# RWKV scan: exponentials wait for less, seeds cross partition halves by transfers

## The chip, the cores and the metric

The kernel runs on one core of a Trainium2 chip. The metric is the device time of one execution in microseconds (us), from start to end, and the median of three runs is given. All data is f32. The core has a matrix engine (PE, whose weight loads are listed apart as PEld), a vector engine (DVE), a scalar engine (ACT), GpSimd (POOL) and SyncE (SP), which here only issues transfers. Each engine works through its own list of instructions in order, and the lists meet by semaphores.

## The reference, cut to what matters

The reference is one step of a four-layer diffusion backbone over 128 context tokens and 1024 latent tokens, width 1024. Layers 0 and 3 mix tokens by a bidirectional RWKV-7 scan, layer 1 by attention, layer 2 by a short convolution. Each layer begins with an RMS norm, scaled and shifted by columns made from a conditioning vector. The scan goes over all tokens, in both directions, for 16 heads with 64x64 states:

```python
def step(S, inp):
    r_t, w_t, k_t, v_t, kk_t, a_t = inp
    sa = jnp.einsum('bdhvk,bdhk->bdhv', S, -kk_t)
    S = (S * w_t[..., None, :] + sa[..., None] * (kk_t * a_t)[..., None, :]
         + v_t[..., None] * k_t[..., None, :])
    return S, jnp.einsum('bdhvk,bdhk->bdhv', S, r_t)
```

## The kernel before, in words

The build runs phase after phase with a barrier between them: `phase_open`, then for each layer its mixer and a boundary phase. The change touches `phase_open` and `phase_scan`; the scan runs twice, for layers 0 and 3.

**The scan.** It does not step token by token. It works on 36 pairs: a pair is one 128-token tile in each direction for two blocks of 128 channels, so four units (two directions, two blocks) of two heads each. Inside a tile the recurrence over 64 tokens is solved by inverting a triangular 64x64 matrix for each unit, head and half tile. The inverse is built by doubling in five levels, n = 2, 4, 8, 16, 32. Of pair q:

- the decayed operands are made ahead: DVE sums the log decays (`decay`, L1625) and subtracts (`decay_before`, L1631), ACT makes five exponentials (`exps(q, 0)` to `exps(q, 4)`, L1516), and DVE multiplies (`decayed_a` L1645, `decayed_b` L1653, `decayed_k` L1658, `decayed_r` L1663).
- `gram(q, t)` (PE, L1286) makes the products of keys with keys and queries, `masked` (DVE, L1677) keeps the triangle, and `pairs(q, t)` (DVE, L1671) puts the entries of the first doubling step into the tile `y1` (semaphore `y1_ok`, two per pair).
- from `y1` come two things. `seeds` (DVE, L1686) transposes its blocks into the tile `x`, from which `level_u(q, 1)` (PE, L1313) starts. `turned_seeds` (PE, L1297) moves its blocks across the two partition halves by eight half-size products with the identity into two PSUM banks, and `copy_seeds` (ACT, L1524) copies them into `xt` (semaphore `t1_ok`), from which `level_x(q, 1)` (PE, L1327) starts.
- level k: `level_u` (PE), `level_w` (DVE, L1698, keeps the entries of this level), `level_x` (PE, L1327), `copy_x` (ACT, L1520, semaphore `xa_ok`), `level_t` (PE, a transposition, L1338), `copy_t` (ACT, L1549, semaphore `xt_ok`).
- `tokens_v`, `tokens_bk` (PE, L1357, L1364) turn values and keys, `values` (PE, L1375) and `copy_values` (ACT, L1543) make a part of the right-hand side.

The states go along in a chain one pair behind: `chain_rhs` (PE L1393 and L1398, DVE L1711), `chain_sa` (PE L1414, ACT L1558), `chain_state` (PE L1425 and L1433, DVE L1736), `chain_y` (ACT, L1567) and the scalings (DVE, L1717).

**The order.** Each engine's list is one loop over q, written out by hand: in iteration q, PE, ACT and DVE do the levels of pair q, both steps of the chain of pair q-1 and the gram of pair q+1, and ACT and DVE prepare pair q+2. ACT's list has, in the first half of iteration q, this stretch:

```python
if chain:
    chain_sa(c, 0)
if nxt2:
    exps(q + 2, 0)
if here:
    copy_values(q)
    copy_x(q, 2)
if chain:
    chain_y(c, 0)
if nxt2:
    exps(q + 2, 1)
```

`exps(q, i)` for i below 4 waits until `decayed_r`, `decayed_a` and `decayed_k` of the pair before are done. Of these, `exps(q, 0)` writes into the tile `er`, which `decayed_r` reads; `exps(q, 1)` and `exps(q, 2)` write into `ab`, which `decayed_a` and the others read. On DVE the order is `decayed_r(q+1)`, `level_w(q, 2)`, `decayed_k(q+1)`, `decay_before(q+2)`, `decayed_a(q+1)`.

PE's list ends iteration q with `level_u(q, 5)`, `level_t(q, 4)`, `turned_seeds(q+1)`, and begins iteration q+1 with `chain_rhs`, `level_u(q+1, 1)`, `tokens_v`, `last_level_t` (L1347), `level_x(q+1, 1)`. ACT has `copy_seeds(q+1)` between `chain_y(c, 1)` and `exps(q+2, 4)`, ahead of `copy_t(q, 4)`. SP issues, in iteration q, the eight loads of pair q+3 (L1113, L1116, L1118, L1126; they wait for pair q+1's products of DVE), once the reload of `g.x` (q = 1, 4608 KB), and the stores of pair q-1's outputs (L1246: two in iterations whose pair is 4 to 19, one before, none after; where SP stores one or none, POOL adds the rest into memory, L1814). Line L1984, which the prediction uses for comparison, stands in the attention phase: eight transfers of 64 KB in a row from 16 partitions to 16 others, both ends in SBUF.

**The opening.** `phase_open` loads x in four parts. ACT squares its eight blocks (L264) into two buffers, PE adds them up over channels by 24 products with a tile of ones, which is loaded (`norm_matmuls`, L333), and each buffer is free when PE has read it. DVE and ACT turn the sums into 1/rms, DVE multiplies x by it (L306). In the same PE list, behind the norm, stand the products of the conditioning vector with the eight pieces of the first layer's weights (`ada_products`, L168; pieces loaded by L246), then a copy by ACT (L184), four transpositions (L176), a sum on DVE (L193, L201), and with these columns ACT and DVE scale and shift (L276, L316), which ends the phase.

Of the kernel before, what the change touches and what calls it, by code (L numbers as in the profile page):

```python
# [20 lines left out]
P = 128  # L21
# [7 lines left out]
CH = 3  # L29
# [182 lines left out]
def phase_open(nc, g, layer):  # L212
# [4 lines left out]
    ms, root, rstd = g.big[0][:, 0, :], g.big[0][:, 1, :], g.extra[:, 0:T]  # L217
    rest = g.arena[:, 2 * NB * T:4 * NB * T]
# [8 lines left out]
    with ExitStack() as ctx:  # L227
        sem = Sems(nc, ctx)
        cond_in, ident_in, ones_in, chan_in, next_in, set_ok, sig_ok, silu_ok = sem(
            "cond_in", "ident_in", "ones_in", "chan_in", "next_in", "set_ok", "sig_ok", "silu_ok")  # L230
        sq_ok, sq_used, ms_ok, root_ok, rstd_ok, tmp_ok, h_ok, h_vector_ok = sem(
            "sq_ok", "sq_used", "ms_ok", "root_ok", "rstd_ok", "tmp_ok", "h_ok", "h_vector_ok")
# [5 lines left out]
        @block.sync  # L238
        def _(sp):
            sp.dma_start(cond, io["cond"]).then_inc(cond_in, 16)  # L240
            n = NB // X_PARTS
            for i in range(X_PARTS):
                sp.dma_start(g.x[:, n * i:n * i + n, :], io["x"][:, n * i:n * i + n, :]).then_inc(x_in[i], 16)
            sp.dma_start(g.ones[:, :], io["ones"]).then_inc(ones_in, 16)
            for k in range(NB):
                sp.dma_start(pieces[k], io["w_ada"][0, k]).then_inc(piece_in[k], 16)  # L246
            sp.dma_start(g.ident[:, :], io["ident"]).then_inc(ident_in, 16)
            sp.dma_start(g.chan[:, :], io["chan"]).then_inc(chan_in, 16)
            sp.dma_start(g.head_ones[:, :], io["head_ones"]).then_inc(next_in, 16)
            for s in range(WSLOTS):  # L250
                sp.dma_start(g.slab[:, s, :], io["w"][mixer_slabs(layer) + s]).then_inc(next_in, 16)
            sp.wait_ge(next_in, 16 * (WSLOTS + 1))

        @block.scalar
        def _(act):
# [4 lines left out]
            for b in range(NB):  # L260
                act.wait_ge(x_in[b * X_PARTS // NB], 16)
                if b >= 2:
                    act.wait_ge(sq_used, b - 1)
                nc.scalar.activation(sq[b % 2], g.x[:, b, :], ACT.Square).then_inc(sq_ok, 1)  # L264
# [4 lines left out]
            act.wait_ge(set_ok, 4)  # L269
# [10 lines left out]
        @block.tensor  # L280
        def _(pe):
            pe.wait_ge(ones_in, 16)
            norm_matmuls(pe, g, sq, sq_ok, sq_used, 0)
            pe.wait_ge(silu_ok, 1)
            for k in range(NB):
                pe.wait_ge(piece_in[k], 16)
                mm = ada_products(pe, g, pieces[k], ROWS, k)
            mm.then_inc(rows_mm, 1)
            pe.wait_ge(ident_in, 16)
            pe.wait_ge(rows_sb, ADA_TILES)  # L290
            ada_turned(pe, g, rows, COLS).then_inc(cols_mm, 1)

        @block.vector
        def _(dve):
# [4 lines left out]
            dve.wait_ge(set_ok, 4)  # L299
            dve.wait_ge(sig_ok, 1)  # L300
            nc.vector.tensor_tensor(g.silu[:, :], cond, sig, op=ALU.mult).then_inc(silu_ok, 1)
            dve.wait_ge(sq_used, NB)
# [23 lines left out]


def norm_matmuls(pe, g, sq, sq_ok, used, banks):

    for b in range(NB):  # L330
        pe.wait_ge(sq_ok, b + 1)
        for c in range(CH):
            mm = pe.matmul(g.ps[:, banks + c, 0:CW], g.ones[:, :], sq[b % 2][:, c * CW:(c + 1) * CW],  # L333
                           start=b == 0, stop=b == NB - 1)
        mm.then_inc(used, 1)
# [804 lines left out]
def phase_scan(nc, g, j):  # L1140
# [46 lines left out]
    with ExitStack() as ctx:  # L1187
# [3 lines left out]
        gram_mm, init_mm, u_mm, x_mm, t_mm, rhs_mm, sa_mm, st_mm, y_mm, tok_mm, rv_mm = sem(  # L1191
            "gram_mm", "init_mm", "u_mm", "x_mm", "t_mm", "rhs_mm", "sa_mm", "st_mm", "y_mm", "tok_mm", "rv_mm")
        g_ok, y1_ok, x_ok, xa_ok, t1_ok, xt_ok, w_ok, rhs_ok, sav_ok, sum_ok, start_ok, half_ok, end_ok, y_ok, tok_ok, tokv_ok, rv_ok = sem(
            "g_ok", "y1_ok", "x_ok", "xa_ok", "t1_ok", "xt_ok", "w_ok", "rhs_ok", "sav_ok", "sum_ok", "start_ok", "half_ok", "end_ok", "y_ok", "tok_ok",
# [3 lines left out]
        ahead_in = sem("ahead_in")  # L1198
        v_in = [sem(f"v_in{i}") for i in range(4)]
# [15 lines left out]
        def _(sp):  # L1215
# [12 lines left out]

            sp.dma_start(w_all, io["scan_const"][:, lay["w"]:]).then_inc(w_in, 16)
# [4 lines left out]
            load(2)  # L1234
            for q in range(PAIRS + 1):
                if q + 3 < PAIRS:
                    load(q + 3)
                if q == 1:
                    sp.wait_ge(g.late_st, 32 * (j + 1))
                    sp.dma_start(g.x[:, :, :], g.x_kept[j]).then_inc(x_in, 16)  # L1240
# [30 lines left out]
        def _(pe):  # L1271
            def gram(q, t):
                if t == 0:
                    pe.wait_ge(b_ok, q + 1)
                    pe.wait_ge(r_ok, q + 1)
                    pe.wait_ge(k_ok, q + 1)
                    pe.wait_ge(a_ok, q + 1)

                    if q:
                        pe.wait_ge(rv_ok, q)  # L1280
                else:
                    pe.wait_ge(y1_ok, 2 * q + 1)
                    pe.wait_ge(g_ok, 4 * q + 2)
# [8 lines left out]
            def turned_seeds(q):  # L1292
                pe.wait_ge(g_ok, 4 * q + 4)
                pe.wait_ge(y1_ok, 2 * q + 2)
                for h in range(2):
                    for p in range(2):
                        mm = pe.matmul(strided(ps, (3 + p) * 512, (1, 256), rows=HALVES[h]), g.ident[HALVES[p], HALVES[p]],  # L1297
                                       strided(y1, h * 256, (1, 256), rows=HALVES[p]), start=True, stop=True)
                mm.then_inc(init_mm, 1)

            def level_u(q, k):
# [5 lines left out]
                else:  # L1307
                    pe.wait_ge(xa_ok, 4 * q + k - 1)
# [9 lines left out]
            def level_x(q, k):  # L1318
                pe.wait_ge(w_ok, 10 * q + 2 * k)
                if k == 1:  # L1320
                    pe.wait_ge(t1_ok, q + 1)
# [10 lines left out]
            def level_t(q, k):  # L1332

                pe.wait_ge(xa_ok, 4 * q + k)
                if q or k > 1:
                    pe.wait_ge(xt_ok, 5 * q + k - 1)
# [15 lines left out]
            def tokens_v(q):  # L1352
                if q:
                    pe.wait_ge(v_in[q % 4], 32 * loads(q, 4))
                pe.wait_ge(t1_ok, q + 1)
# [24 lines left out]
            def chain_rhs(c, step):  # L1380
# [4 lines left out]
                if c or step:  # L1385
                    pe.wait_ge(y_ok, 2 * c + step)
                    pe.wait_ge(sav_ok, 4 * c + 2 * step)
# [50 lines left out]
            for q in range(-1, PAIRS + 1):  # L1438
# [44 lines left out]
                if nxt:  # L1483
                    turned_seeds(q + 1)
# [3 lines left out]
        def _(act):  # L1488
# [12 lines left out]
            def exps(q, i):  # L1501
                act.wait_ge(cum_ok, q + 1)
                if i in (1, 4):
                    act.wait_ge(d0_ok, q + 1)
                if q and i < 4:
                    act.wait_ge(r_ok, q)
                    act.wait_ge(a_ok, q)
                    act.wait_ge(k_ok, q)
# [12 lines left out]

            def copy_seeds(q):
                act.wait_ge(init_mm, q + 1)
                A.copy(strided(xt[q % 2], 0, (P, 2), (256, 2), (1, P)),  # L1524
                       strided(ps, 3 * 512, (512, 2), (P, 2), (1, P))).then_inc(t1_ok, 1)
# [44 lines left out]
            for q in range(-2, PAIRS + 1):  # L1570
# [40 lines left out]
                if nxt:  # L1611
                    copy_seeds(q + 1)
# [7 lines left out]
        def _(dve):  # L1620
# [45 lines left out]
            def pairs(q, t):  # L1666
                p = HALVES[1 - t]
                dve.wait_ge(gram_mm, 4 * q + 2 * t + 2)
                if q and t == 0:
                    dve.wait_ge(init_mm, q)  # L1670
# [1108 lines left out]
def constants():  # L2779
# [33 lines left out]
    out["ones"] = np.ones((P, P), np.float32)  # L2813
# [92 lines left out]
```

## Time and profile before

| | us |
|---|---|
| median of three runs | 4566.91 (4566.62 to 4568.85) |
| the profiled execution, its own time | 4574.58 |
| its span, first to last instruction | 4572.7 |
| first scan, about | 651 to 1400 |
| second scan, about | 3650 to 4400 |
| opening, about | 0 to 54.7 |

A row of the time line gives the start in us, the duration in us, the engine, the line, the operation, the tiles (output <- input), shapes and count; in brackets stands how long the engine had been idle before and who released it. A row of one line's instructions gives the count and the minimum, median and maximum duration in ns. A row of waits gives us in total, times, and the longest.

### The profile page before, as it was taken

The page shows a single profiled execution, that of the slowest core. Times are in us where ns is not written, and L with a number is a line of the kernel's source. Part 1 is how long each engine was busy: PE and PEld are TensorE (multiplying, and loading weights), DVE is VectorE, ACT ScalarE, POOL GpSimd, SP SyncE. Part 2 cuts the span into 40 slices and gives each one's busy share as a digit, 9 for nine tenths or more (in the row PEclk, how much of TensorE's full clock was granted, in tenths as well). Part 3 has the DMA queues.
Part 4 walks back from the last instruction along what each step waited for, and adds up shares of the span by engine and source line. Part 5 has one row for each costly group of instructions (what it writes and reads, how often), then busy time and mean ns, then how long its engine had stood idle before and what let it go on. Part 6 is the DMA issues. An engine that isn't in the chain of part 4 may idle for free. (4 is left out here: it accounts for less than half of the span.)

```text
span 4572.7 us, 133471 instructions
## 1 busy us (share of the span) xinstructions
PE 4107.4 (90%) x58784; PEld 3528.4 (77%) x58784; DVE 2634.2 (58%) x4521; ACT 1943.5 (43%) x3640; POOL 92.4 (2%) x82
## 2 busy tenths in 40 slices
PE   6999978998887899899998999889999788888978
PEld 2888867877775799666668899877988677777758
DVE  5433557777775643355556433467425477777755
ACT  5333325555554531455554000145333255555542
POOL 0000000000110000000000000000000000001100
PEclk9999989999998899899999999999999889999989
DMA  7444765334434131100000221112346843334341
GB/s 300 147 129 130 223 197 144 93 94 101 98 75 160 69 73 43 53 1 1 1 16 23 97 97 67 53 62 69 118 133 187 250 129 103 99 88 100 86 152 61
DMA packets 541152, 471.09 MB, mean 103 GB/s; under 512 B 30113, under 2 KB 501409, under 8 KB 532897
## 3 DMA queue, kind: packets, MB, share of 16 engines
q1 hardware_dynamic: 389152, 387.03, 26.6%
q10 hardware_dynamic: 131840, 66.07, 5.0%
q0 software_dynamic: 19584, 9.44, 2.2%
q8 instruction: 468, 7.67, 0.7%
q14 instruction: 108, 0.88, 0.1%
HBM read 328.50 MB, written 128.71 MB: 100 GB/s over the span
## 5 line engine op out<-in xcount | busy, mean ns | idle before, releaser
L654 PE MATMUL ps<-big_r,stage_r 128*128 128x384 f32 x2976 | 640.0, 350 | 15.7 <-DVE big_r L916 14.3
L654 PEld LDWEIGHTS ps<-big_r,stage_r 128*128 128x128 f32 x2976 | 522.3, 189 | 71.0 <-issue 25.7
L2559 PE MATMUL ps<-big_r,w_out 128*128 128x384 f32 x2304 | 417.5, 341 | 35.9 <-DVE w_out L2675 35.4
L2559 PEld LDWEIGHTS ps<-big_r,w_out 128*128 128x128 f32 x2304 | 406.6, 191 | 45.0 <-DVE w_out L2675 38.6
L654 PE MATMUL ps<-big_r,w_slab_r 128*128 128x384 f32 x1488 | 341.3, 337 | 0.0
L371 PE MATMUL ps<-big_r,stage_r 128*128 128x384 f32 x1536 | 311.0, 337 | 13.7 <-DVE big_r L358 13.6
L1698 DVE COPY_PREDICATED arena<-arena,ps 128x128 f32<-128x128 uint32 x720 | 195.1, 328 | 207.1 <-PE ps L1313 204.6
L2281 DVE TENSOR_REDUCE extra<-ps 128x1 f32<-128x1152 f32 (+1 forms) x144 | 177.7, 1234 | 204.7 <-PE ps L2186 204.7
L371 PEld LDWEIGHTS ps<-big_r,stage_r 128*128 128x128 f32 x1536 | 269.8, 188 | 29.1 <-issue 26.7
L1338 PE MATMUL ps<-ident,arena 128*128 128x128 f32 x1152 | 186.7, 285 | 103.9 <-ACT arena L1520 103.2
L654 PEld LDWEIGHTS ps<-big_r,w_slab_r 128*128 128x128 f32 x1488 | 268.0, 189 | 0.0
L1520 ACT COPY arena<-ps 128x512 f32<-128x512 f32 x288 | 169.3, 588 | 209.7 <-PE ps L1327 209.7
L1327 PE MATMUL ps<-arena 64*64 64x64 f32 x9216 | 225.5, 227 | 16.5 <-issue 13.8
L770 ACT ACTIVATE x_resid<-ps,chan 128x384 f32<-128x384 f32 x192 | 101.2, 578 | 294.8 <-PE ps L692 293.7
L1338 PEld LDWEIGHTS ps<-ident,arena 128*128 128x128 f32 x1152 | 125.3, 141 | 127.4 <-ACT arena L1520 122.1
L1286 PE MATMUL ps<-arena 64*128 64x128 f32 x2304 | 179.3, 296 | 44.6 <-DVE arena L1645 35.8
L1327 PEld LDWEIGHTS ps<-arena 64*64 64x64 f32 x9216 | 181.9, 136 | 42.5 <-issue 20.6
L2207 PE MATMUL ps<-ident,arena 128*128 128x128 f32 x1168 | 188.7, 285 | 27.7 <-ACT arena L2266 20.9
L1516 ACT ACTIVATE arena<-arena 128x256 f32<-128x256 f32 (+2 forms) x360 | 159.6, 465 | 123.8 <-DVE arena L1645 116.6
L2256 ACT ACTIVATE arena<-ps,extra 128x1152 f32<-128x1152 f32 (+1 forms) x144 | 162.2, 1126 | 73.3 <-DVE extra L2281 69.2
L1286 PEld LDWEIGHTS ps<-arena 64*128 64x128 f32 x2304 | 149.6, 197 | 56.2 <-issue 48.7
L2207 PEld LDWEIGHTS ps<-ident,arena 128*128 128x128 f32 x1168 | 122.8, 141 | 82.2 <-issue 53.1
(257 smaller groups left out, 8046.0 us busy)
## 6 DMA issues: line engine op xcount, KB each, us to landing
w_slab<-in_w SPq DMA_DIRECT2D x138, 512.0 KB, 3.5
arena<-scan_in SPq DMA_DIRECT2D x144, 320.0 KB, 3.7
arena<-scan_in SPq DMA_DIRECT2D x288, 128.0 KB, 3.8
scan_in<-x_resid ACTq DMA_DIRECT2D x48, 576.0 KB, 4.6
arena<-scan_in SPq DMA_DIRECT2D x48, 576.0 KB, 6.7
arena<-scan_in SPq DMA_DIRECT2D x144, 192.0 KB, 3.9
arena<-in_w_ada SPq DMA_DIRECT2D x24, 1024.0 KB, 6.0
x_resid<-in_w_ada SPq DMA_DIRECT2D x24, 1024.0 KB, 4.9
```

Of the source, the lines that this page charges most:

```text
L371: mm = pe.matmul(g.ps[:, bank + c, 0:CW], w[:, k * P:(k + 1) * P], x[:, k, c * CW:(c + 1) * CW], start=k == i == 0, stop=k == NB - 1 and i ...
L654: mm = pe.matmul(g.ps[:, 3 * s + c, 0:CW], w[:, k * P:(k + 1) * P], x[:, k, chunk(c)], start=k == i == 0, stop=k == NB - 1 and i == 2)
L1286: mm = pe.matmul(strided(ps, (3 + h) * 512 + u * P, (1, P)), strided(bk[q % 2], u * 256 + t * P, (1, P), rows=HALVES[h]), strided(ar[q % 4 ...
L1327: mm = pe.matmul(strided(ps, h * 512 + (2 * d + s) * HD, (1, HD), rows=HALVES[p]), strided(xt[q % 2], lx(d, p, s), (1, HD), rows=HALVES[h] ...
L1338: mm = pe.transpose(strided(ps, 2 * 512 + lx(d, 0, s), (P, 2), (1, HD)), strided(x, (2 * d + s) * P, (1, P)), g.ident[:, :])
L1516: A.activation(out, src, ACT.Exp, scale=sign).then_inc(exp_ok, 1)
L1520: A.copy(strided(x, 0, (HD, 2), (P, 4), (1, HD)), strided(ps, 0, (512, 2), (HD, 4), (1, HD))).then_inc(xa_ok, 1)
L1698: V.copy_predicated(strided(wk(k), p * P, (256 + n, 2), (2 * n, HD // n), (1, n)), bits(strided(level_mask, (k - 1) * P, (HD, 2), (n, HD / ...
L2207: mm = pe.transpose(g.ps[:, bank, i * P:(i + 1) * P], prob[n % 2][h][:, (3 * k + i) * P:(3 * k + i + 1) * P], g.ident[:, :])
L2256: A.activation(prob[n % 2][h][:, 0:width(n)], scored(n, h), ACT.Exp, bias=nmax[n % 2][h], accum_out=rsum[n % 2][h]).then_inc(exp_ok, 1)
L2281: V.tensor_reduce(nmax[n % 2][h], scored(n, h), mybir.AxisListType.X, ALU.max, negate=True).then_inc(max_ok, 1)
L2559: mm = pe.matmul(g.ps[:, bank(i, b), 0:wide[i]], w[:, b, k * P:(k + 1) * P], r, start=k == j == 0, stop=k == NB - 1 and j == 2)
```

## The change

In the scan, `exps(q, 0)` waits for the sums and for `decayed_r` of the pair before only; `exps(q, 1)` waits for `decay_before` and `decayed_a` of the pair before; the later ones wait for nothing of their own. PE loses waits: in `gram`, `level_u`, `level_t` and `chain_rhs`. `turned_seeds` leaves PE and `copy_seeds` leaves ACT; in their place SP issues four transfers of 64 KB each from `y1` to `xt`, from each half of the partitions to each half, behind the load of pair q+3 and ahead of the store of pair q-1. They wait for `pairs(q+1, 1)`, and `level_x(q+1, 1)` waits for their landing. `tokens_v` and the next `pairs` wait accordingly. In the opening, the tile of ones is set by DVE and not loaded, DVE adds the squares of the eight blocks into one tile by seven sums, and PE makes three products of it, not 24.

The diff, cut to its core:

```diff
@@ phase_open
+    total = g.big[0][:, 2, :]
...
-            sp.dma_start(g.ones[:, :], io["ones"]).then_inc(ones_in, 16)
...
                 if b >= 2:
-                    act.wait_ge(sq_used, b - 1)
+                    act.wait_ge(added_ok, max(b - 2, 1))
                 nc.scalar.activation(sq[b % 2], g.x[:, b, :], ACT.Square).then_inc(sq_ok, 1)
...
-            pe.wait_ge(ones_in, 16)
-            norm_matmuls(pe, g, sq, sq_ok, sq_used, 0)
+            pe.wait_ge(set_ok, 5)
+            pe.wait_ge(added_ok, NB - 1)
+            for c in range(CH):
+                pe.matmul(g.ps[:, c, 0:CW], g.ones[:, :], total[:, c * CW:(c + 1) * CW], start=True, stop=True).then_inc(sum_mm, 1)
...
-            dve.wait_ge(sq_used, NB)
+            for b in range(1, NB):
+                dve.wait_ge(sq_ok, b + 1)
+                if b > 1:
+                    dve.wait_ge(added_ok, b - 1)
+                nc.vector.tensor_tensor(total, sq[0] if b == 1 else total, sq[b % 2], op=ALU.add).then_inc(added_ok, 1)
+            dve.wait_ge(sum_mm, CH)
...
@@ phase_scan, SP
+            def turned_seeds(q):
+                sp.wait_ge(y1_ok, 2 * q + 2)
+                if q >= 2:
+                    sp.wait_ge(sa_mm, 2 * (q - 2) + 2)
+                for h in range(2):
+                    for p in range(2):
+                        sp.dma_start(strided(xt[q % 2], p * P, (256, 2), (1, P), rows=HALVES[h]),
+                                     strided(y1, h * 256, (P, 2), (1, P), rows=HALVES[p])).then_inc(t1_ok[q % 2], 16)
...
             load(2)
+            turned_seeds(0)
             for q in range(PAIRS + 1):
                 if q + 3 < PAIRS:
                     load(q + 3)
+                if q + 1 < PAIRS:
+                    turned_seeds(q + 1)
...
@@ phase_scan, PE
             def gram(q, t):
                 if t == 0:
-                    pe.wait_ge(b_ok, q + 1)
-                    pe.wait_ge(r_ok, q + 1)
-                    pe.wait_ge(k_ok, q + 1)
                     pe.wait_ge(a_ok, q + 1)
...
-            def turned_seeds(q):
-                pe.wait_ge(g_ok, 4 * q + 4)
-                pe.wait_ge(y1_ok, 2 * q + 2)
-                for h in range(2):
-                    for p in range(2):
-                        mm = pe.matmul(strided(ps, (3 + p) * 512, (1, 256), rows=HALVES[h]), g.ident[HALVES[p], HALVES[p]],
-                                       strided(y1, h * 256, (1, 256), rows=HALVES[p]), start=True, stop=True)
-                mm.then_inc(init_mm, 1)
...
-                else:
-                    pe.wait_ge(xa_ok, 4 * q + k - 1)
+                if k == 5:
+                    pe.wait_ge(xa_ok, 4 * q + 4)
...
                 if k == 1:
-                    pe.wait_ge(t1_ok, q + 1)
+                    pe.wait_ge(t1_ok[q % 2], 64 * (q // 2 + 1))
...
-                pe.wait_ge(xa_ok, 4 * q + k)
-                if q or k > 1:
-                    pe.wait_ge(xt_ok, 5 * q + k - 1)
+                if k < 4:
+                    pe.wait_ge(xa_ok, 4 * q + k)
+                if q and k == 1:
+                    pe.wait_ge(xt_ok, 5 * q)
...
-                pe.wait_ge(t1_ok, q + 1)
+                pe.wait_ge(y1_ok, 2 * q + 2)
...
-                    pe.wait_ge(sav_ok, 4 * c + 2 * step)
...
-                if nxt:
-                    turned_seeds(q + 1)
@@ phase_scan, ACT
             def exps(q, i):
-                act.wait_ge(cum_ok, q + 1)
-                if i in (1, 4):
+                if i == 0:
+                    act.wait_ge(cum_ok, q + 1)
+                    if q:
+                        act.wait_ge(r_ok, q)
+                if i == 1:
                     act.wait_ge(d0_ok, q + 1)
-                if q and i < 4:
-                    act.wait_ge(r_ok, q)
-                    act.wait_ge(a_ok, q)
-                    act.wait_ge(k_ok, q)
+                    if q:
+                        act.wait_ge(a_ok, q)
...
-            def copy_seeds(q):
-                act.wait_ge(init_mm, q + 1)
-                A.copy(strided(xt[q % 2], 0, (P, 2), (256, 2), (1, P)),
-                       strided(ps, 3 * 512, (512, 2), (P, 2), (1, P))).then_inc(t1_ok, 1)
...
-                if nxt:
-                    copy_seeds(q + 1)
@@ phase_scan, DVE, pairs
                 if q and t == 0:
-                    dve.wait_ge(init_mm, q)
+                    dve.wait_ge(t1_ok[(q - 1) % 2], 64 * ((q - 1) // 2 + 1))
```

## Rows read from the trace of the kernel before

**Rows 1.** First scan's busy us: stage, length, PE, PEld, DVE, ACT, POOL; clock, DMA share, GB/s.

```profile
660.00:1360.00 700.00, 623.08 (x20196) 544.51 (x20194) 536.47 (x1149) 406.77 (x934) 39.09 (x32) 0.99 0.39 101
```

**Rows 2.** Waits in 900 to 1300 us, first scan: us in total, times, longest.

```profile
PEld ps L1338 <- ACT arena L1520: 34.6, 40, 1.7
...
ACT arena L1516 <- DVE arena L1645: 27.9, 20, 1.4
```

**Rows 3.** Time line of one iteration, first scan, around the first exponential.

```profile
1006.24 0.68 DVE L1663 TENSOR_TENSOR arena<-arena 128x512 f32<-128x512 f32 x1
...
1008.74 0.69 DVE L1645 TENSOR_TENSOR arena<-arena 128x512 f32<-128x512 f32 x1
...
1008.82 0.98 PE L1433 MATMUL ps<-arena 128*64 128x64 f32 x16
...
1009.60 0.42 ACT L1516 ACTIVATE arena<-arena 128x256 f32<-128x256 f32 x1 [1.42 <-DVE arena L1645]
...
1010.38 0.59 ACT L1520 COPY arena<-ps 128x512 f32<-128x512 f32 x1
...
1011.02 0.42 PEld L1338 LDWEIGHTS ps<-ident,arena 128*128 128x128 f32 x4 [1.36 <-ACT arena L1520]
...
1014.70 0.42 PEld L1338 LDWEIGHTS ps<-ident,arena 128*128 128x128 f32 x4 [0.38 <-ACT arena L1520]
```

**Rows 4.** Time line where that iteration begins, around the turned seeds.

```profile
1000.04 0.72 DVE L1671 COPY_PREDICATED arena<-arena,ps 64x512 f32<-64x512 uint32 x1
...
1000.65 0.66 PE L1338 MATMUL ps<-ident,arena 128*128 128x128 f32 x4
...
1001.23 0.66 PE L1297 MATMUL ps<-arena,ident 64*64 64x256 f32 x8
1001.44 0.71 DVE L1686 STREAM_TRANSPOSE arena<-arena 128x512 f32<-128x512 f32 x1 [0.16 <-PE ps L1338]
...
1002.21 0.67 PE L1313 MATMUL ps<-arena,stage 64*64 64x32 f32 x32
...
1004.15 0.13 PEld L1327 LDWEIGHTS ps<-arena 64*64 64x64 f32 x1
```

**Rows 5.** Transfers: lines L1984 and L1246 with their landings; time line of SP and POOL.

```profile
L1984 SPq DMA_DIRECT2D arena<-arena x80: 507/589/2022, 1597.5 to 1732.2; - x80
...
DMA to landing us min/median/max: 2.2/2.3/3.7
...
L1246 SPq DMA_DIRECT2D scan_y<-arena x72: 359/360/1546, 698.5 to 4084.9; - x72
...
DMA to landing us min/median/max: 1.8/1.9/11.8
...
1010.42 1.43 SPq L1116 DMA_DIRECT2D arena<-scan_in  x1
...
1013.45 1.00 SPq L1126 DMA_DIRECT2D arena<-scan_in  x2
...
1258.28 2.44 POOL L1814 DMA_DIRECT2D scan_y<-arena  x2 [18.10 <-ACT arena L1567]
```

**Rows 6.** The opening: time line, and line L246 with its landings.

```profile
15.47 17.65 PE L333 MATMUL ps<-stage,ones 128*128 128x384 f32 x48 [15.47 <-DMA ones<-in_ones]
...
33.05 7.05 PE L168 MATMUL ps<-arena,silu 128*2 128x512 f32 x64
...
36.94 10.24 DVE L306 TENSOR_TENSOR arena<-x_resid,extra 128x1152 f32<-128x1152 f32 x8 [2.42 <-ACT extra L268]
...
42.74 0.64 PE L176 MATMUL ps<-ident,arena 128*128 128x128 f32 x4 [2.65 <-ACT arena L184]
...
47.52 4.01 DVE L316 TENSOR_SCALAR arena<-arena,ada 128x128 f32<-128x128 f32 x8
...
L246 SPq DMA_DIRECT2D arena<-in_w_ada x8: 437/590/2369, 3.8 to 10.5; - x8
...
DMA to landing us min/median/max: 14.1/20.8/24.8
```

More of the change, by code:

```diff
@@ L228, in phase_open @@
         sem = Sems(nc, ctx)
[L229 to L232, printed above, removed]
+        cond_in, ident_in, chan_in, next_in, set_ok, sig_ok, silu_ok = sem(
+            "cond_in", "ident_in", "chan_in", "next_in", "set_ok", "sig_ok", "silu_ok")
+        sq_ok, added_ok, sum_mm, ms_ok, root_ok, rstd_ok, tmp_ok, h_ok, h_vector_ok = sem(
+            "sq_ok", "added_ok", "sum_mm", "ms_ok", "root_ok", "rstd_ok", "tmp_ok", "h_ok", "h_vector_ok")
         rows_mm, rows_sb, cols_mm, cols_sb, vec_ok = sem("rows_mm", "rows_sb", "cols_mm", "cols_sb", "vec_ok")
@@ L268, in _ @@
             nc.scalar.activation(rstd, root, ACT.Exp, scale=-0.5).then_inc(rstd_ok, 1)
-            act.wait_ge(set_ok, 4)
+            act.wait_ge(set_ok, 5)
             act.wait_ge(rows_mm, 1)
@@ L298, in _ @@
             nc.vector.memset(rows, 0.0).then_inc(set_ok, 1)
-            dve.wait_ge(set_ok, 4)
+            nc.vector.memset(g.ones[:, :], 1.0).then_inc(set_ok, 1)
+            dve.wait_ge(set_ok, 5)
             dve.wait_ge(sig_ok, 1)
             nc.vector.tensor_tensor(g.silu[:, :], cond, sig, op=ALU.mult).then_inc(silu_ok, 1)
-            dve.wait_ge(sq_used, NB)
+            for b in range(1, NB):
[4 more added lines that the diff above has]
+            dve.wait_ge(sum_mm, CH)
             nc.vector.tensor_scalar(as3(ms), slot_view(g.ps[:, 0:3, :]), 1.0 / D, RMS_EPS, ALU.mult, ALU.add).then_inc(ms_ok, 1)
@@ L324, in token_ranges @@
     return ((0, 0, CTX), (1, CTX, T))
[L328 to L335, printed above, removed]
 def take_high(nc, dst, src):
@@ L1190, in phase_scan @@
             "x_in", "w_in", "init_in", "state_st", "zero_ok", "cum_ok", "d0_ok", "exp_ok", "bb_ok", "a_ok", "b_ok", "t_ok", "kd_ok", "k_ok", "r_ok", "less_ok")
[L1191 to L1194, printed above, removed]
+        gram_mm, u_mm, x_mm, t_mm, rhs_mm, sa_mm, st_mm, y_mm, tok_mm, rv_mm = sem(
+            "gram_mm", "u_mm", "x_mm", "t_mm", "rhs_mm", "sa_mm", "st_mm", "y_mm", "tok_mm", "rv_mm")
+        g_ok, y1_ok, x_ok, xa_ok, xt_ok, w_ok, rhs_ok, sav_ok, sum_ok, start_ok, half_ok, end_ok, y_ok, tok_ok, tokv_ok, rv_ok = sem(
+            "g_ok", "y1_ok", "x_ok", "xa_ok", "xt_ok", "w_ok", "rhs_ok", "sav_ok", "sum_ok", "start_ok", "half_ok", "end_ok", "y_ok", "tok_ok",
             "tokv_ok", "rv_ok")
@@ L1198, in phase_scan @@
         ahead_in = sem("ahead_in")
+        t1_ok = [sem(f"t1_ok{i}") for i in range(2)]
         v_in = [sem(f"v_in{i}") for i in range(4)]
@@ L1281, in gram @@
                 else:
-                    pe.wait_ge(y1_ok, 2 * q + 1)
                     pe.wait_ge(g_ok, 4 * q + 2)
@@ L2812, in constants @@
     out["ident"] = np.eye(P, dtype=np.float32)
-    out["ones"] = np.ones((P, P), np.float32)
     out["head_ones"] = (row // HD == col // HD).astype(np.float32)
```

## The prediction, made before the changed kernel was run

> **What bounds the kernel now.** I read three views, in this order: busy time by stage, the waits, and the time line of one iteration. The busy times say that no engine is full in the scan: PE works 623 of 700 us and DVE 536 [rows 1]. At most 77 us of each scan are PE's idle time, so what counts is which wait stands on the path and what is behind it in the same list. The waits name one that comes once per pair: ACT is idle 20 times in 400 us before its exponential line, 27.9 us in all, 1.4 each, and the one it waits for is the product L1645 (`decayed_a`) [rows 2]. PE's transposition L1338 waits for ACT's copy L1520 40 times there, twice per pair, 34.6 us [rows 2].
>
> The time line shows that the second is made by the first. ACT has been free since 1009.60 - 1.42 = 1008.18, but the next in its list is `exps(q+2, 0)`, which waits until `decayed_a` ends at 1008.74 + 0.69 = 1009.43. Behind it stand two copies; the second, `copy_x(q, 2)`, ends at 1010.97, and PE's `level_t(q, 2)` starts at 1011.02 after 1.36 idle [rows 3]. The other wait of L1338 in the pair is 0.38 [rows 3], so the first one is on average (34.6 - 20 x 0.38) / 20 = 1.35 us, and it is on the path, since PE is busy on both sides of it.
>
> At the seam of two iterations the reader should see something else: the turned seeds lie in a shadow. `level_t(q, 4)` ends at 1001.31, DVE's `seeds` runs from 1001.44 to 1002.15, and `level_u` of the next pair starts at 1002.21, 0.06 after it. PE's eight products of the turned seeds (0.66, from 1001.23) fall into that turn-around of DVE [rows 4].
>
> **The change part by part.**
>
> *Exponentials.* Freed of `decayed_a`, `exps(q+2, 0)` needs `decayed_r`, done at 1006.92 [rows 3], so it starts when ACT is free, at 1008.18. It and the two copies took 1009.60 to 1010.97, 1.37 us; now they end at 1009.55. PE's step before `level_t` ends at 1009.80 [rows 3], so PE no longer waits: 1.35 less the 0.05 of a hand-off gives 1.30 per pair. `exps(q+2, 1)`, which now carries the wait for `decayed_a`, comes behind `chain_y`, whose products end at 1009.80, after 1009.43: it waits for nothing new, and behind it `copy_t(q, 2)` has over a microsecond in hand. Next late is DVE's `level_w(q, 3)`, which waits for PE and moves with it. 34 iterations of each scan have such an exponential ahead of this wait: 68 x 1.30 = **88 us less**.
>
> *Other waits taken from PE and ACT.* Each is implied by one that stays on the same engine, so none came last. What an instruction that waits costs is not shown alone; PE follows its releaser by 0.06 with two waits in front [rows 4], which bounds it. Some six places per pair give between 0 and 0.36 x 72 = 26 us; I take 0, since PE's list runs ahead of its array while that is busy [rows 1]. A loss is excluded here.
>
> *Turned seeds off PE and ACT.* 0.66 us of PE and a copy of ACT go, but `level_u` starts when `seeds` is done, so the gain is at most 1002.21 - 1002.15 = 0.06 per pair [rows 4]; I take 0. PE waits there instead.
>
> *Turned seeds as transfers.* `pairs(q+1, 1)` ends at 1000.76 and `level_x` starts at 1004.15 [rows 4]: what comes by 3.34 us after `y1` (0.05 for the hand-off) costs nothing, and each microsecond beyond it moves PE's whole list, for the engine is in order and `level_x` heads it. The path is 0.05 to SP, three issues, and issue to landing of the fourth. No row is this transfer, so two bound it. By size, place and number the nearest is L1984 (64 KB, SBUF to SBUF, in a row): 0.59 per issue, 2.3 to landing [rows 5], so 0.05 + 1.77 + 2.3 = 4.12, 0.78 late. By shape (many rows, 512-byte pieces) the nearest is the store L1246: 0.36 and 1.9 [rows 5], so 0.05 + 1.08 + 1.9 = 3.03, in time. I take the middle, 3.58: 0.24 late. On top, an issue on SP now and then takes one microsecond more, as 1.43 against some 0.5 [rows 5]; one in eight does in the load of this iteration, none in others, so for four issues I allow 0.3. And in the last 16 pairs of each scan POOL's adding transfers begin at the same moment [rows 5] and share the engines of the transfers: from 0 to 0.7 more in 32 of 72, on average I take 0.1. Together 0.6 late per pair, 71 x 0.6 = **43 us more**; the ends are 0 and 0.78 + 0.3 + 0.3 = 1.4, 0 to 99 us.
>
> The rule that speaks against this edit: the Trainium skill, DMA: Bandwidth & Descriptors, Rules for kernel authors, says that two transfers to disjoint halves of the partitions are not worth splitting, because they run on the same engines and serialize. In this trace eight such transfers, each 2.3 us to landing, are issued at 0.59 apiece, so they overlap. The section Anatomy of one DMA puts the fixed part at about 2.0 us (for POOL's path); with 0.15 for 64 KB, an estimate from that page, the middle above would come out 0.05 later.
>
> *What else SP is moved past.* The stores of pair q-1 go behind four issues, some 2 us later; their buffer is written again one and a half iterations on, so 0. The load of pair q+3 stands ahead: its last two issues run from 1013.45 to 1014.45 and, at 2.3 to 3.7 from issue to landing [rows 5], it ends by some 1016.3 to 1017.7. A pair takes 19 to 20 us (20 waits in 400 us [rows 2]), so `y1` of the next pair, 1.3 earlier than now, comes at 1000.76 + 19 - 1.3 = 1018.5 or later. That margin is thin; a queue there is in the upper end. The reload of x in iteration 1 goes behind the seeds of pair 2: 0.
>
> *Opening.* The 24 products run until 33.12 because the tile of ones comes at 15.47 [rows 6]. In their place stand seven sums on DVE of 10.24 / 8 = 1.3 us: even begun as late as 15.47 they end at 24.6, with three products by 25.6, and DVE's multiplications, which start 36.94 - 33.12 = 3.8 after the products and take 10.24, by 39.6. Next late are the pieces of weights: the last is issued at 10.5 and lands 24.8 later, at 35.3 at the latest. Its share of L168 is 7.05 / 8 = 0.9, so the products end at 36.2, not 40.1; from there to the end of the transpositions was 3.3 us, from which the columns follow 0.4 later: 40.0 in place of 47.52 [rows 6]. If PE, then little used, runs at the lower clock, one microsecond comes back. **7 us less**, between 5 and 8.
>
> Sum: -88 + 43 - 7 = **-52 us**. The profiled execution took 4574.6 (span 4572.7), 7.7 above the median of 4566.9; the sum goes from execution to execution alike, so I set it on the median: 4566.9 - 52 = **4515**.
>
> **The rivals.**
>
> *The transfers are hidden.* If they cost what the stores cost, `t1` comes at 3.03 and the whole gain stays: -95, 4472. For it: the shape, and that PE is itself late at this place in some iterations. Against: the SBUF transfers in the trace are the slower ones.
>
> *The seeds become the bound (slower).* Should the landing be like the slowest shown for L1984, 3.7 us [rows 5], at 0.59 per issue, they come at 0.05 + 1.77 + 3.7 = 5.52, 2.2 late, and 71 x 2.2 = 156 less 95 gives +61: 4628. It decides from 95 / 71 = 1.34 late. Strictly one after the other, as the skill's rule reads, they would come at 0.05 + 4 x 2.3 = 9.25, 5.9 late: 419 less 95, 4891. Against both: 2.3 is the median of 80, and eight are issued in a row.
>
> *A new wait eats the exponentials' gain.* DVE is busy 77% [rows 1], and if it or ACT follows PE by only half, 44 us stay: -44 + 43 - 7 = -8, 4559. That would also be the picture if `exps(q+2, 0)` still waited, for `decayed_r`; but that one is done 1.3 before ACT is free.
>
> **How the numbers follow.** About 0.2% (9 us) is what a measurement can tell from no change. The forecast has 0.62, the hidden transfers 0.2, the half gain 0.1, late seeds 0.07, the strict sequence 0.01. The range goes from the hidden case with a little lateness (0.1 late, -95 + 7: 4479) to 1.2 late (-95 + 85: 4557). Faster by over 0.2%: the first two and part of the third, 0.86; within it 0.07; slower 0.07.
>
> **What would show it.** ACT's exponential L1516 should have no wait for L1645, and L1338 one wait per pair of about 0.4 in place of two. PE should show a short wait, some 0.3 to 0.9, before `level_x` of level 1, released by a transfer; longer in the last 16 pairs. A pair should take about 0.7 us less; the columns of the opening should be there near 40. The prediction is wrong if that transfer wait is over 1.34, or if the 1.3 us shows up again before another step of PE.

## The result, and the profile after

The changed kernel is slower: 4616.07 us (median of 4 runs, 4613.37 to 4626.67) against 4567.88 of the kernel before on the same chip, a ratio of 1.0109 [1.0092, 1.0127]. That is 48 us more, where 52 less were forecast. The profiled execution is the slowest of the four, 4626.67 with a span of 4624.9. "Pair" below is an iteration of the scan, 36 in each of two scans.

The time line of the changed kernel, around the seam of pairs 16 and 17 of the first scan and the first exponential behind it (start, duration, engine, line; in brackets the idle time before and who ended it). L1660 is now `pairs`, L1234 the transfers, L1324 `level_x`, L1336 `level_t`, L1512 `exps`, L1516 `copy_x`:

```profile
995.31 0.73 DVE L1660 COPY_PREDICATED arena<-arena,ps 64x512 f32<-64x512 uint32 x1
...
996.07 3.34 SPq L1234 DMA_DIRECT2D arena<-arena  x4
...
996.72 0.71 DVE L1675 STREAM_TRANSPOSE arena<-arena 128x512 f32<-128x512 f32 x1 [0.16 <-PE ps L1336]
...
1000.98 0.59 PEld L1324 LDWEIGHTS ps<-arena 64*64 64x64 f32 x32 [1.30 <-issue]
1001.01 0.69 PE L1324 MATMUL ps<-arena 64*64 64x64 f32 x32 [1.19 <-DMA arena<-arena]
...
1004.11 0.76 ACT L1549 COPY arena<-ps 64x256 f32<-64x256 f32 x2 [0.24 <-PE ps L1411]
...
1004.77 0.41 ACT L1512 ACTIVATE arena<-arena 128x256 f32<-128x256 f32 x1
...
1005.55 0.58 ACT L1516 COPY arena<-ps 128x512 f32<-128x512 f32 x1
...
1006.18 0.42 PEld L1336 LDWEIGHTS ps<-ident,arena 128*128 128x128 f32 x4 [0.17 <-ACT arena L1516]
```

Two things are to be seen. The exponential L1512 starts as soon as ACT is done with L1549, and PE's `level_t` behind it waits 0.17 in place of 1.36 [rows 3]. And `y1` is done at 996.04, but `level_x` starts at 1000.98, 4.94 later; before, it started 3.39 later [rows 4]. The waits in 660 to 1360 us, the first scan, say the same of all its pairs (us in total, times, longest; "issue" is idle time in which the engine waited for nothing that the profile names):

```profile
PEld ps L1324 <- issue: 64.6, 47, 3.4
...
PE ps L1324 <- DMA arena<-arena: 50.4, 30, 3.0
...
PEld ps L1336 <- ACT arena L1516: 16.9, 53, 0.8
```

So does the line of the transfers in the whole kernel (min/median/max in ns; who waited for it, us and times; us to landing):

```profile
L1234 SPq DMA_DIRECT2D arena<-arena x288: 590/608/2210, 653.9 to 4409.3; - x144
...
  PE ps L1324: 121.1, 69
...
DMA to landing us min/median/max: 2.0/2.6/5.3
```

PE now waits for the transfers 69 times, 121.1 us in all. The engine's weight loads, which come first, show the whole stall: 167.8 us idle before L1324 (in the seam of [rows 4] there is none):

```profile
L1324 PEld LDWEIGHTS ps<-arena 64*64 64x64 f32 x9216 | 174.9, 139 | 167.8 <-issue 146.1 <-DVE arena L1687 3.0
```

Busy time of the first scan, in the stretch of [rows 1] (PE, PEld, DVE, ACT, POOL; clock, DMA share, GB/s):

```profile
660.00:1360.00 700.00, 608.99 (x19185) 532.58 (x19184) 518.93 (x1109) 380.33 (x874) 34.27 (x29) 0.95 0.43 110
```

Less work fits into the same 700 us, and the mean granted clock is 0.95 in place of 0.99: more of the stretch ran at 1.2 GHz, the rest at 2.4. A second profile of the changed kernel (g4, shown with f4 below) has 0.98, so this difference is not a firm one.

The opening went as forecast. Its time line (L309 the sums, L285 the products, L168 the last piece of weights, L324 the columns):

```profile
11.69 8.67 DVE L309 TENSOR_TENSOR arena<-arena,stage 128x1152 f32<-128x1152 f32 x6 [1.29 <-ACT stage L264]
...
20.51 3.83 PE L285 MATMUL ps<-arena,ones 128*128 128x384 f32 x6 [20.51 <-DVE arena L309]
...
35.09 1.89 PE L168 MATMUL ps<-arena,silu 128*2 128x512 f32 x8 [1.49 <-DMA arena<-in_w_ada]
...
41.26 4.01 DVE L324 TENSOR_SCALAR arena<-arena,ada 128x128 f32<-128x128 f32 x8
```

The columns start at 41.26 in place of 47.52 [rows 6].

### The profile page after: what moved, and what is told of

Same layout as the page of the kernel before. It is cut to its first block and busy times, and to the rows that moved or that the text cites. A ratio compares the mean times of both kernels' runs of the same rounds, so it can differ in the third digit from the quotient of the medians.

```text
span 4624.9 us, 131604 instructions
## 1 busy us (share of the span) xinstructions
PE 4110.3 (89%) x58166; PEld 3532.7 (76%) x58166; DVE 2643.6 (57%) x4529; ACT 1912.9 (41%) x3568; POOL 92.4 (2%) x82
## 5 line engine op out<-in xcount | busy, mean ns | idle before, releaser
L1324 PE MATMUL ps<-arena 64*64 64x64 f32 x9216 | 215.7, 230 | 136.8 <-DMA arena<-arena 121.1
L1516 ACT COPY arena<-ps 128x512 f32<-128x512 f32 x288 | 168.6, 585 | 331.6 <-PE ps L1324 331.4
L1324 PEld LDWEIGHTS ps<-arena 64*64 64x64 f32 x9216 | 174.9, 139 | 167.8 <-issue 146.1
L1336 PE MATMUL ps<-ident,arena 128*128 128x128 f32 x1152 | 194.1, 293 | 20.1 <-ACT arena L1516 18.9
L1310 PE MATMUL ps<-arena 64*64 64x32 f32 x7680 | 166.9, 224 | 23.5 <-DVE arena L1675 16.9
L2196 PEld LDWEIGHTS ps<-ident,arena 128*128 128x128 f32 x1168 | 122.9, 141 | 82.3 <-issue 53.1
L1310 PEld LDWEIGHTS ps<-arena 64*64 64x64 f32 x7680 | 139.1, 137 | 60.3 <-issue 31.5
```

The source lines that it names most:

```text
L1310: mm = pe.matmul(strided(ps, p * 512 + u * 32, (1, 32), rows=HALVES[h]), strided(gr[q % 3], (1 - p) * 1024 + h * 512 + u * P, (1, HD), row ...
L1324: mm = pe.matmul(strided(ps, h * 512 + (2 * d + s) * HD, (1, HD), rows=HALVES[p]), strided(xt[q % 2], lx(d, p, s), (1, HD), rows=HALVES[h] ...
L1336: mm = pe.transpose(strided(ps, 2 * 512 + lx(d, 0, s), (P, 2), (1, HD)), strided(x, (2 * d + s) * P, (1, P)), g.ident[:, :])
L1516: A.copy(strided(x, 0, (HD, 2), (P, 4), (1, HD)), strided(ps, 0, (512, 2), (HD, 4), (1, HD))).then_inc(xa_ok, 1)
L2196: mm = pe.transpose(g.ps[:, bank, i * P:(i + 1) * P], prob[n % 2][h][:, (3 * k + i) * P:(3 * k + i + 1) * P], g.ident[:, :])
```

## The experiments

The chips differ a little: beside the runs that follow, the kernel before took 4578 to 4585. So every time stands with its ratio to the kernel before on the same chip, and a difference of ratios times 4568 gives the us.

**Undo the transfers** (e1, and again as g3 beside the changed kernel itself as g4, on one chip). In the changed kernel the turned seeds are PE's products and ACT's copy again:

```diff
-                if q + 1 < PAIRS:
-                    turned_seeds(q + 1)        # SP: four transfers
...
+                if nxt:
+                    turned_seeds(q + 1)        # PE: eight products
...
+                if nxt:
+                    copy_seeds(q + 1)          # ACT
```

> The changed kernel with the turned seeds back on PE and ACT; exponentials, other waits and opening as changed. Theory (the transfers come late and PE stands before level_x; all else gained as worked out): 4568 - 88 (exponentials) - 6 (opening, read off the trace of after) = about 4474, ratio to before 0.979; level_x of level 1 starts 3.4 us after y1. Rival (the exponentials' gain is given back at another wait, and the transfers cost little): 4540 to 4565.

> The kernel of e1 once more, beside g2 on the same chip. If the opening's 6 us add: g2 less 6, ratio 0.0014 below g2. If e1's 16 us came from its chip: as f2 less 6, ratio 0.985.

> The changed kernel once more, on the chip of g2 and g3, for the cost of the transfers on one chip: g4 less g3. By the lateness of level_x in the traces (1.7 us x 71 = 121, of which some is taken up by stalls that PE has anyway): 95 to 120 us; ratio to before 1.009 to 1.013.

e1 took 4534.09, ratio 0.9882 [0.9861, 0.9904]; g3 4516.80, 0.9875 [0.9860, 0.9889]; g4 4626.61, 1.0110 [1.0094, 1.0126]. So the transfers cost (1.0109 - 0.9882) x 4568 = 104 us, and 4626.6 - 4516.8 = 110 on one chip: all that was lost, and more. But without them the rest gives only 54 to 61, where e1's theory had 94; e1 lies outside its rival's range too. The idle time of PE's weight loads before `level_x` (here L1321) falls to 43.4, about what it was in the kernel before (42.5):

```profile
L1321 PEld LDWEIGHTS ps<-arena 64*64 64x64 f32 x9216 | 183.9, 138 | 43.4 <-issue 22.2 <-DVE arena L1693 3.6
```

167.8 - 43.4 = 124 us are the stall itself. The net cost is 14 to 20 smaller, and other stalls of PE shrink beside it: all idle gaps of its weight loads over 0.25 us in the two scans come to 239 us in the changed kernel and 138 in e1, a difference of 101.

**Undo the exponentials' waits in the changed kernel** (e2).

```diff
             def exps(q, i):
-                if i == 0:
-                    act.wait_ge(cum_ok, q + 1)
-                    if q:
-                        act.wait_ge(r_ok, q)
-                if i == 1:
+                act.wait_ge(cum_ok, q + 1)
+                if i in (1, 4):
                     act.wait_ge(d0_ok, q + 1)
-                    if q:
-                        act.wait_ge(a_ok, q)
+                if q and i < 4:
+                    act.wait_ge(r_ok, q)
+                    act.wait_ge(a_ok, q)
+                    act.wait_ge(k_ok, q)
```

> The changed kernel with the old waits of the exponentials. Theory: their 1.3 us per pair come back beside the late transfers, 4616 + 88 = about 4704, and L1336 again waits 1.3 us once per pair. Rival (with the seeds late, the exponentials' wait has no weight any more, because DVE's products move less than PE): 4616 to 4640.

4732.81, 1.0314 [1.0291, 1.0337]: (1.0314 - 1.0109) x 4568 = 94 us. The idle time of PE's weight loads before `level_t`, in e2 and in the changed kernel:

```profile
L1336 PEld LDWEIGHTS ps<-ident,arena 128*128 128x128 f32 x1152 | 137.8, 151 | 132.0 <-ACT arena L1515 127.2
```

```profile
L1336 PEld LDWEIGHTS ps<-ident,arena 128*128 128x128 f32 x1152 | 132.8, 147 | 40.9 <-ACT arena L1516 35.1
```

The new waits do what they were read to do: 132.0 - 40.9 = 91 us of this wait are gone.

**Two of the four transfers early** (e3). The two that read the half of `y1` that is written first are issued before the other half is there: 3.4 and 2.7 us before `y1` is complete (medians), where in the changed kernel all four are issued 0.03 to 1.97 us or more after it:

```diff
-                sp.wait_ge(y1_ok, 2 * q + 2)
-                if q >= 2:
-                    sp.wait_ge(sa_mm, 2 * (q - 2) + 2)
-                for h in range(2):
-                    for p in range(2):
+                for p in (1, 0):
+                    sp.wait_ge(y1_ok, 2 * q + 2 - p)
+                    if p and q >= 2:
+                        sp.wait_ge(sa_mm, 2 * (q - 2) + 2)
+                    for h in range(2):
```

> The changed kernel with two of the four transfers of a pair issued already after the first half of y1, some 5 us earlier; two are left behind the second half. Theory (number of issues times 0.62 plus 2.1 to landing, plus an instruction fetch): the last one is issued 0.65 after y1 instead of 2.0 to 2.8, level_x starts at about 4.0 instead of 5.5, 71 x 1.4 = 100 us less, about 4516. Rival (the landing is held by instruction fetches and POOL's transfers, whatever the issue): level_x stays above 5, less than 40 us gained, 4576 or more.

4518.06, 0.9851 [0.9824, 0.9877], as the theory expected. The line of the transfers in that kernel:

```profile
  PE ps L1324: 10.5, 21
...
DMA to landing us min/median/max: 2.0/2.6/4.3
```

A single transfer lands no sooner (median 2.6 in both), but PE waits for it 21 times, 10.5 us, not 69 times, 121.1. With two issues fewer in front, the last of the group is issued 0.66 after `y1`, and what still delays its landing is mostly over before PE needs the seeds.

**POOL's adding transfers held back** (e4): in the last 14 pairs that have them they wait until the seeds have landed.

```diff
                 pool.wait_ge(y_st[c % 2], stored_by(c))
+                if MEET <= c and c + 2 < PAIRS:
+                    pool.wait_ge(t1_ok[c % 2], 64 * ((c + 2) // 2 + 1))
```

> The changed kernel with POOL's adding transfers of pairs 20 to 33 held back until the seeds of that moment have landed. If they hold the seeds up by the 1 us by which the last 16 pairs are later than the others: 28 x 1 = 28 us less, about 4588, and level_x at 5.0 in the late pairs as in the early ones. If they do not: 4616.

4603.84 (10 runs), 1.0038 [1.0026, 1.0051]: (1.0109 - 1.0038) x 4568 = 32 us less than the changed kernel. Its line of the transfers:

```profile
  PE ps L1324: 89.7, 69
...
DMA to landing us min/median/max: 2.0/2.3/3.9
```

The waits fall by the same 121.1 - 89.7 = 31 us, the median of the landings from 2.6 to 2.3.

**Both** (f3 = e3 and e4 together), beside **the kernel before again** (f1), with a profile, for its trace on that chip:

> Two early transfers and POOL's adding transfers held back, together. If the two lateness terms add: the late pairs' level_x falls from 4.08 to about 3.75, 28 x 0.35 = 10 us less than e3, ratio 0.983. If e3 already had the transfers out of the way: as e3, 0.985.

> The kernel before, once more, for a trace from the same chip as the three next to it. Its scans should come out as long as on record (697 and 700 us between the first and the last y1) if the chip does not matter, some 10 us longer if it does.

f3 took 4490.14, 0.9807 [0.9786, 0.9827] (0.983 expected), the fastest of all: 91 us below the kernel before on its chip (4581.54), and below the version with the seeds on PE, whose interval begins at 0.9860. Its time line shows the four transfers spread over 4.60 us, and POOL's, which now wait for them:

```profile
1199.71 4.60 SPq L1234 DMA_DIRECT2D arena<-arena  x4
...
1207.27 2.44 POOL L1805 DMA_DIRECT2D scan_y<-arena  x2 [17.31 <-DMA arena<-arena]
```

f1 took 4580.24.

**The exponentials alone** in the kernel before (f2), and **with PE's dropped waits** (g2; the `wait_ge` lines that the change takes out of `gram`, `level_u`, `level_t` and `chain_rhs`, no more):

```diff
             def exps(q, i):
-                act.wait_ge(cum_ok, q + 1)
-                if i in (1, 4):
+                if i == 0:
+                    act.wait_ge(cum_ok, q + 1)
+                    if q:
+                        act.wait_ge(r_ok, q)
+                if i == 1:
                     act.wait_ge(d0_ok, q + 1)
-                if q and i < 4:
-                    act.wait_ge(r_ok, q)
-                    act.wait_ge(a_ok, q)
-                    act.wait_ge(k_ok, q)
+                    if q:
+                        act.wait_ge(a_ok, q)
```

> The kernel before with the new waits of the exponentials alone. The first theory, the prediction's, gives 88 us less, ratio 0.981. The theory after e1 (the wait goes, but PE then stands for its instruction fetches and at a lower granted clock, and half of the gain is given back): 35 to 50 us less, ratio 0.989 to 0.992, the same as e1 less its opening's 6.

> The kernel of f2 (exponentials' waits) and in addition the waits that the change takes from PE; turned seeds and opening as before. The prediction took these waits at nothing: as f2, ratio 0.987. Rival, after e1 came out 16 us above f2 less the opening: they cost 10 to 20 us, ratio 0.990 to 0.991.

f2: 4519.83, 0.9867 [0.9847, 0.9888]. g2: 4519.08, 0.9868 [0.9852, 0.9885]. The exponentials alone give (1 - 0.9867) x 4568 = 61 us, between the two expectations (88, and 35 to 50), and PE's dropped waits nothing that these runs resolve. Where the rest of the 88 went is in the idle times of PE's weight loads. First the kernel before (f1), then f2:

```profile
L1313 PEld LDWEIGHTS ps<-arena 64*64 64x64 f32 x7680 | 139.7, 136 | 34.1 <-issue 27.7 <-ACT arena L1520 1.7 <-DVE arena L1686 0.7
...
L1338 PEld LDWEIGHTS ps<-ident,arena 128*128 128x128 f32 x1152 | 126.4, 142 | 125.3 <-ACT arena L1520 119.6 <-issue 1.3
...
L1313 PEld LDWEIGHTS ps<-arena,stage 64*64 64x64 f32 x3840 | 69.1, 134 | 22.0 <-issue 20.1
```

```profile
L1313 PEld LDWEIGHTS ps<-arena 64*64 64x64 f32 x7680 | 140.6, 135 | 48.2 <-issue 42.1 <-ACT arena L1521 1.7 <-DVE arena L1687 0.7
...
L1338 PEld LDWEIGHTS ps<-ident,arena 128*128 128x128 f32 x1152 | 125.1, 141 | 41.2 <-ACT arena L1521 31.5 <-issue 3.3
...
L1313 PEld LDWEIGHTS ps<-arena,stage 64*64 64x64 f32 x3840 | 71.1, 136 | 26.4 <-issue 24.5
```

Before `level_t` (L1338) 125.3 - 41.2 = 84 us are gone, which is the forecast's term. But before `level_u` (L1313) there are 14.1 + 4.4 = 18.5 more, all of it "issue". What that is can be seen where such a stall cuts a row of equal instructions in two. In f2, the weight loads of one step of the chain (L1414), and what the DMA engines did at that time (packets, MB, share of the 16 engines):

```profile
1212.72 0.19 PEld L1414 LDWEIGHTS ps<-arena 64*64 64x64 f32 x2
1214.56 0.32 PEld L1414 LDWEIGHTS ps<-arena 64*64 64x64 f32 x14 [1.65 <-issue]
```

```profile
q1 hardware_dynamic: 1252, 0.60, 90.6%
q8 instruction: 1, 0.02, 2.3%
```

No semaphore stands between the second and the third of these sixteen loads. One instruction packet came in while the loads of a later pair held the DMA engines, and PE went on 1.41 after its end. Counting all gaps of PE's weight loads over 0.25 us in the two scans, those that end 1.2 to 1.75 us after such a packet are 98 of 225 (80.6 us) in f1 and 121 of 197 (93.5 us) in f2; by chance it would be one in eight. The other two profiles say the same: 77.8 us in the first one of the kernel before, 96.2 in g2. And of the 93.5 us, 56 stand behind the 70 of 320 packets that came in while the DMA engines were 80% busy or more; in f1 it was 23 behind 61. So, by their timing, a wait on the path had hidden some 13 us of PE's instruction fetches; with the wait gone they stand in the open. No run takes the packets away.

**The opening alone** in the kernel before (g1; the parts of the diff in `phase_open`):

> The kernel before with the new opening alone. By the trace of after its columns are there 6.3 us earlier: 6 us less, ratio 0.9986. If the opening costs something later (a colder PE): ratio 1.000 or above.

4567.06 (10 runs), 0.9976 [0.9967, 0.9985]: 11 us less [7, 15], where the time line gives 6.3. But on top of the other changes this gain does not show: g3 has the new opening and g2 has not, and g3 is no lower (0.9875 against 0.9868), so both values expected for g3, 0.9854 and 0.985, were missed. The two intervals leave room for a gain of some 6 us, hardly for 11.

**The wait filled** (f4). Eight transpositions of the identity, whose result nothing reads, stand on PE before `level_x` of level 1, so that PE works while the transfers are on their way:

```diff
+            def filler():
+                for u in range(8):
+                    pe.transpose(strided(ps, 4 * 512 + (u % 4) * P, (1, P)), g.ident[:, :], g.ident[:, :])
...
+                if here:
+                    filler()
                 if here:
                     level_x(q, 1)
```

> The changed kernel with eight transpositions of the identity (1.3 us) put into PE's list ahead of level_x of level 1, into a PSUM bank that is free there; their result is used by nothing. Theory (part of the loss is the granted clock, which falls after PE's idle stretches): half-clock time in the scans falls from 96 us to below 50 and the kernel gets 10 to 30 us faster, ratio 1.004 to 1.009. Rival (the clock costs nothing, the transfers' lateness is all): same as after or slower by the overshoot where the seeds come before 4.7, ratio 1.011 to 1.015.

4619.05, 1.0083 [1.0058, 1.0109]. Its busy times in the same stretch, and behind them those of the changed kernel run again (g4):

```profile
660.00:1360.00 700.00, 629.79 (x19514) 547.88 (x19516) 519.60 (x1112) 380.56 (x877) 34.95 (x30) 0.99 0.43 110
```

```profile
660.00:1360.00 700.00, 602.50 (x19288) 525.44 (x19286) 521.73 (x1116) 381.20 (x878) 36.65 (x30) 0.98 0.44 110
```

With the filling the mean granted clock is 0.99, but without it it was 0.95 once and 0.98 the other time, so that PE's standing still costs clock is not shown. The ratio is 0.0026 lower (12 us), which the intervals don't separate from nothing. Clock is at most a small part of the loss.

## Why the prediction was wrong

**The step that failed is the transfers' price.** "I take the middle, 3.58: 0.24 late", plus 0.3 for SP's issues and 0.1 for POOL, put the seeds 3.98 after `y1`. From the end of L1660 to the first weight load of L1324 the time lines give, as a mean of 72 pairs, 3.67 before, 3.80 in e1, and 5.52 after. Each of the three parts was too small (pairs are numbered from 0 in each scan):

- *The transfers by themselves.* In four of the first 20 pairs of the two scans neither an issue nor the last landing is held, and there `level_x` starts 4.08 to 4.19 after `y1` (pair 18 of the first scan: 1016.15 to 1020.23). L1984 gave 4.12: by size, place and number it was the nearest row, and the one to go by. Averaging it with a store to HBM, near only by shape, lost 0.5. These are that pair's DMA queues and issues (KB each, median us to landing):

```profile
q1 hardware_dynamic: 722, 0.34, 33.8%
issues: line engine op xcount, KB each, median us to landing
arena<-arena SPq DMA_DIRECT2D x4, 64.0 KB, 2.0
```

- *Instruction packets.* This had no term of its own. The page of the changed kernel counts them, and PE's instructions:

```profile
PE 4110.3 (89%) x58166; PEld 3532.7 (76%) x58166; DVE 2643.6 (57%) x4529; ACT 1912.9 (41%) x3568; POOL 92.4 (2%) x82
...
q8 instruction: 461, 7.55, 0.7%
```

58166 x 2 / 461 = 252 instructions of PE to a packet of 16 KB. 314 of them fall into the scans, 4.4 a pair, each on one DMA engine for a median of 1.05 us, and in all but a few pairs one falls among the seeds: an issue is held, or the last landing comes late. This is pair 17, with `level_x` 4.94 after `y1`; its packet ends 2.32 after `y1`, and the fourth issue starts at 2.76:

```profile
q8 instruction: 1, 0.02, 1.2%
issues: line engine op xcount, KB each, median us to landing
arena<-arena SPq DMA_DIRECT2D x4, 64.0 KB, 2.6
```

  In the first 20 pairs of a scan the mean is 5.04, some 0.9 over an undisturbed pair; 0.3 was allowed. The trace ties both delays to the packet: each of the 31 issues of L1234 that took over 0.8 us ended 0.38 to 0.45 after the end of a packet; and of the first 20 pairs of the two scans 18 have such an issue, while 18 others have none and their last landing comes 1.06 to 1.50 after the end of a packet. No run tests it by taking the packets away.

- *POOL.* In the last 16 pairs the mean is 6.11, 1.07 more. In pair 27 all three meet, and the median landing is 3.3:

```profile
q0 software_dynamic: 544, 0.26, 44.8%
q1 hardware_dynamic: 576, 0.26, 19.5%
q8 instruction: 1, 0.02, 1.4%
...
arena<-arena SPq DMA_DIRECT2D x4, 64.0 KB, 3.3
```

  Over all pairs that is 1.07 x 32 / 72 = 0.48; 0.1 was taken, and "0 to 0.7" as the bound did not hold it. e4 shows this cause: with POOL held back, 32 us go.

3.98 + 0.5 + 0.6 + 0.4 = 5.5. The seeds are 5.52 - 3.80 = 1.72 later than from PE, on 72 pairs 124 us, which is the stall of L1324; 104 to 110 of it reached the end. By the prediction's own count they are 5.52 - 3.34 = 2.2 late, over the 1.34 at which the rival "the seeds become the bound" decides, and it is this rival that came about (4628 forecast, 4616 measured). That its price, 5.52, is the measured mean is luck: its reason was a landing of 3.7 in every pair, and the traces show packets and POOL holding issues and landings by amounts that differ from pair to pair. Its total is near because two errors cancel: it had 156 us for the transfers, where 104 to 110 reached the end, and 95 for the rest, where 54 to 61 did. It had a chance of 0.07 because 2.3 was the median of L1984; but the step waits for the last of four, and that is set by the slow ones.

**The exponentials' term was right at its place and too big in the sum.** L1338's wait fell by 84 of 88 us, the exponentials wait no more for the product; alone it gave 61 (the interval is 51 to 70). Of the 27 missing, 4 were not there to gain, and 18.5 stand before `level_u`, which by their timing are mostly PE's fetches; the rest is within the scatter. All idle gaps over 0.25 us of PE's weight loads say the same: they fall from 196 us in f1 to 132 in f2, by 64. The rival "a new wait eats the gain" kept 44 of 88, and it looked to DVE and ACT, but what was lost stood on PE. With the transfers in, the same edit is worth 94: there 91 us go before `level_t` (e2), and before `level_u` (L1310) only 6.5 more stand. Why the fetches show less there stays open.

**Right:** the opening (7; 6.3 by the time line, 11 by g1); PE's dropped waits at 0, as far as these runs resolve it (g2 equals f2); and SP's place in the order: the first transfer is issued 0.03 after `y1` in all 72 pairs, so the load of pair q+3 was never in its way. The turned seeds off PE, taken at 0, no run tests by themselves.

The sum by the measured terms is -61 - 11 + 107 = 35, against 48 [42, 58] measured. The 107, between 104 and 110, were taken with all else in place, so the gap is in the other two: together they gave 54 to 61 (e1, g3), not 72.

**The rule weighed in the prediction.** Undisturbed, four transfers issued 0.65 apart (an issue of 0.61 and a gap) were all there 2.0 after the start of the last issue (pair 18), so they overlap; one after the other, at 2.0 each, would have been 8. The Trainium skill, DMA: Bandwidth & Descriptors, Rules for kernel authors, says that transfers to disjoint halves serialize; the trace does not agree as to time. Its reason is that all share the same 16 engines, and that fits what the runs show: one packet of 1 us, and POOL's transfers (e4), hold them. The same page of the Trainium skill, Anatomy of one DMA, puts the fixed part at about 2.0 us for POOL's path; the shortest landing here, on SP's, is 2.0.

## What to carry to other kernels

A transfer that an in-order engine waits for is priced by the last of its group and by the traffic that shares its engines (other queues' bursts and the engines' own instruction packets), not by the median of a quiet row; the nearest row by size, place and number is to be taken, not a mean with a farther one. Moving work from a full engine to DMA pays when the issue can stand several microseconds ahead of the need: here the same four transfers cost 104 to 110 us when all came behind the last half of their data, and beat the products they replace when two of them were issued some 3 us before that half and POOL was held back. And a wait that is taken off the path gives less than its length where it hid other stalls: look at "issue" gaps of the steps next to it.

## What was unexpected of the hardware

- *Instruction fetches show twice.* By their timing, they stop PE (93.5 us in the scans of f2, with 121 stops, each ended 1.2 to 1.75 us after a 16 KB packet), most of all while loads fill the DMA engines (56 of the 93.5); and they delay small transfers (0.9 us on average in the first 20 pairs). The Trainium skill, Runtime: NRT & Kernel Launch, Instruction fetch mechanics, tells of blocks of 16 KiB with 256 instructions, which fits the 252 above, and calls the cost mostly hidden; in f2 a stop stands behind 121 of the 320 packets of the scans.
- *A held issue.* An issue of L1234 takes some 0.6 us, but the fourth starts 2.2 to 3.6 after `y1` in place of 1.97 in 22 of 72 pairs: in most of them the one before it was held, for up to 2.21, and its issue ended some 0.4 after the end of an instruction packet.
- *Clock.* The mean granted clock of the same stretch differs from profile to profile of one kernel: 0.99 and 0.97 (f1) before, 0.95 and 0.98 (g4) after. One profile doesn't settle such a difference, and the 0.99 with eight idle transpositions (f4) is no proof that they brought it back.
